# Query splits two groups ahead, a ring of two for the K products, early prompt rows, and a compression loop that runs through sample boundaries

## The reference, cut to what matters

```python
q, kvc_rows, kvs_rows, kvw_rows, gl, u = project_in(h, p['w_in'])
kv_c, cmp_end = cmp_finish(cmp_partials(kvc_rows, p['w_cmp']), p['pe_cmp'], p['w_cmp'])
# cmp_partials: blocks of 16 rows times weights, two halves r
return jnp.einsum('bnsxhd,xrsde->rbnxhe', sub, w)
# for each sample the rows of the compressed branch come through a page table
kvc_past = cache_kv_cmp[layer, page_table].reshape(bd, past_len, 2, N_KV_HEADS, HEAD_DIM)
```

## Time and profile before

| | us |
|---|---|
| median of 3 runs | 1994.75 |
| lowest and highest run | 1992.07, 1998.62 |
| profiled execution, its own time | 1998.57 |
| span of the profiled execution, first to last instruction | 1996.9 |
| PE busy in the span | 1787.3 (90%) |
| projection, from its first matmul to its last | 36.25 to 287.4 |
| compression, from its first transpose to the first of the attention | 288.2 to 427.2 |
| attention, to the first transpose of the next stage | 427.2 to 888.9 |
| rest: SSM, output projection, FFN, final norm | 888.9 to 1996.9 |

### The profile page before, as it was taken

One profiled execution on the slowest core, in us unless ns is written; L12 is line 12 of the kernel. 1 busy time (PEld: TensorE's weight loads), 2 busy tenths in 40 slices (PEclk: granted clock), 3 DMA queues, 4 the chain that ended last, 5 costly groups with the idle time before them and its releaser, 6 DMA issues. The chain is left out here.

```text
span 1996.9 us, 27094 instructions
## 1 busy us (share of the span) xinstructions
PE 1787.3 (90%) x10875; PEld 1502.0 (75%) x10876; DVE 915.0 (46%) x1404; ACT 567.9 (28%) x876; POOL 307.6 (15%) x265
## 2 busy tenths in 40 slices
PE   5999788856998999886869979999999999999988
PEld 4655778854555554545649979999999999999977
DVE  3456004673544443417121055555555555555554
ACT  4000013553443343320221133232222222222222
POOL 0000000022212211210011012222222222222210
PEclk8999897977999999896989979999999999999999
DMA  6312414401333322536010021112111111211102
GB/s 257 65 43 107 157 49 153 164 39 53 96 95 112 121 85 86 197 134 199 4 63 22 1 75 40 55 32 63 32 60 35 34 61 32 63 32 57 37 11 90
DMA packets 94796, 155.15 MB, mean 78 GB/s; under 512 B 19670, under 2 KB 72446, under 8 KB 92366
## 3 DMA queue, kind: packets, MB, share of 16 engines
q1 hardware_dynamic: 81200, 93.82, 14.7%
q0 software_dynamic: 12672, 58.73, 8.8%
q10 hardware_dynamic: 848, 1.54, 0.3%
HBM read 133.61 MB, written 24.83 MB: 79 GB/s over the span
## 5 line engine op out<-in xcount | busy, mean ns | idle before, releaser
L2224 PE MATMUL ps<-h_up,w_split 128*128 128x344 f32 x2112 | 403.5, 323 | 9.2 <-DVE h_rest L2394 7.4
L2403 DVE TENSOR_TENSOR xT<-ps,xT 128x1032 f32<-128x1032 f32 x176 | 216.9, 1233 | 316.8 <-PE ps L2224 316.8
L2224 PEld LDWEIGHTS ps<-h_up,w_split 128*128 128x128 f32 x2112 | 344.1, 189 | 20.1 <-issue 16.5
L2224 PE MATMUL ps<-gated,wd_split 128*128 128x344 f32 x1584 | 266.8, 324 | 3.0 <-POOL wd_split L2380 2.1
L2224 PEld LDWEIGHTS ps<-gated,wd_split 128*128 128x128 f32 x1584 | 250.5, 188 | 12.7 <-DVE xT L2403 7.8
L2224 PE MATMUL ps<-h_rest,w_split 128*128 128x344 f32 x1056 | 225.0, 321 | 0.0
L2224 PEld LDWEIGHTS ps<-h_rest,w_split 128*128 128x128 f32 x1056 | 179.5, 190 | 0.0
L2410 DVE SCALAR_TENSOR_TENSOR cv<-hu,ccol,cv 128x1024 f32<-128x1024 f32 x88 | 142.7, 1622 | 16.4 <-ACT cv L2322 10.7
L2320 ACT ACTIVATE hu<-ps 128x1032 f32<-128x1032 f32 x44 | 45.4, 1033 | 331.9 <-PE ps L2224 331.9
L2360 POOL TENSOR_TENSOR w_split<-w_raw,w_split 128x1024 fp32r<-128x1024 f32 x44 | 107.0, 2433 | 188.1 <-ACT w_split L2305 188.1
L1601 DVE TENSOR_REDUCE top<-ps 128x1 f32<-128x384 f32 (+4 forms) x124 | 71.3, 586 | 139.4 <-PE ps L1226 73.6
(11 more groups left out here) (436 smaller groups left out, 2514.1 us busy)
## 6 DMA issues: line engine op xcount, KB each, us to landing
w_raw<-in_w_up SPq DMA_DIRECT2D x44, 512.0 KB, 6.1
wd_raw<-in_w_down SPq DMA_DIRECT2D x22, 512.0 KB, 3.6
unit<-in_cache_kv_win POOLq DMA_DIRECT2D x16, 512.0 KB, 4.6
x_kept<-xT SPq DMA_DIRECT2D x1, 4128.0 KB, 25.4
xT<-x_kept SPq DMA_DIRECT2D x1, 4128.0 KB, 19.6
xtok<-in_x_prompt SPq DMA_DIRECT2D x2, 2048.0 KB, 8.1
w_qu<-in_w_in SPq DMA_DIRECT2D x2, 2048.0 KB, 8.6
w_out_sb<-in_w_out SPq DMA_DIRECT2D x4, 1024.0 KB, 5.0
```

What stands on the lines that cost most here:

```text
L2224: mm = pe.matmul(k.ps[:, bank + c, 0:TG], w(wn), x(xn)[:, c * TG:c * TG + TG], start=start and m == 0, stop=stop and m == 2)
L2403: dve.tensor_tensor(x, k.ps[:, bank:bank + 3, 0:TG], x, ALU.add).then_inc(added, 1)
```

## The change

1. **Splits.** "split" of groups 0 and 1 stand at the head of `ORDER`; "split" of g + 2 stands in group g ahead of "value" of the selected branch, instead of at the head of group g + 1.
2. **K products.** `kk_stage` has two places, each with a semaphore of its own; the copy of product x waits for the store of product x - 2. The eight loads of `w_c` go from SP's list to POOL's, into another place in SBUF, behind `cw_made` and the store `pb_kept`.
3. **Prompt rows.** Tile 0 has a place of its own (`tile0`), and SP loads it at the end of its list in the projection, behind the K products' stores and `cw_kept`. `uc_early` moves to the place of sample buffer 0. So gather 2, which writes there, waits for the store `u_kept`.
4. **Compression.** PE, ACT and DVE run one loop over all 72 fills; the combine of tile j - 1 comes after the copy of fill 1 of tile j. Copies of `uc_early` alternate between ACT and DVE.

```diff
+    k.kk_out = [nc.alloc_semaphore(f"kk_out{n}") for n in range(2)]
...
-            for x in range(2):
-                for r in range(2):
-                    for s2 in range(2):
-                        src = k.dram["w_cmp"][0][x, r * SUB + s2:(r + 1) * SUB:2].rearrange("s d e -> d s e")
-                        sp.dma_start(k.w_c[HD * s2:HD * s2 + HD, x, :, r, :], src).then_inc(k.wc_loaded, 16)
             for x in range(KK_FILLS):
                 sp.wait_ge(kk_added, x + 1)
-                sp.dma_start(k.kk_kept[:, 8 * P * x:8 * P * x + 8 * P], k.kk_stage[:].rearrange("c g q -> c (g q)")).then_inc(k.kk_out, 16)
+                sp.dma_start(k.kk_kept[:, 8 * P * x:8 * P * x + 8 * P], k.kk_stage[:, x % 2].rearrange("c g q -> c (g q)")
+                             ).then_inc(k.kk_out[x % 2], 16)
+
+            sp.wait_ge(k.cw_out, 16)
+            for x in range(2):
+                for h in range(NKV):
+                    sp.dma_start(k.tile0[NSUBP:NSUBP + 2, :, 2 * x + h, :],
+                                 k.dram["pe_cmp"][0, x].rearrange("(r s) d -> r s d", r=2)).then_inc(k.prompt_in, 16)
+            sp.wait_ge(*k.cmp_rows_stored)
+            sp.dma_start(k.tile0[0:NSUBP].rearrange("n s c d -> n (s c d)"),
+                         k.dram["p_kv_cmp"][0, 0].rearrange("(n s) x h d -> n (s x h d)", s=SUB)).then_inc(k.prompt_in, 16)
...
+            pool.wait_ge(cw_made, 1)
+            pool.wait_ge(k.pb_out, 16)
+            for x in range(2):
+                for r in range(2):
+                    for s2 in range(2):
...
+                        pool.dma_start(k.w_c[HD * s2:HD * s2 + HD, x, :, r, :], src).then_inc(k.wc_loaded, 16)
...
-                    if x:
-                        act.wait_ge(k.kk_out, 16 * x)
-                    else:
+                    if x >= 2:
+                        act.wait_ge(k.kk_out[x % 2], 16 * (x // 2))
+                    elif x == 0:
...
-            sp.wait_ge(u_moved, 8)
-            sp.wait_ge(k.kk_out, 16 * 4)
+            sp.wait_ge(u_act, 4)
+            sp.wait_ge(u_dve, 4)
             sp.dma_start(k.u_kept, k.uc_early[:].rearrange("p g n -> p (g n)")).then_inc(k.u_spilled, 16)
...
-                if j >= 2:
+                if j == 2:
+                    pool.wait_ge(k.u_spilled, 16)
+                if j >= 3:
 
                     pool.wait_ge(transposed, FILLS * (j - 1))
...
+            for F in range(FILLS * (NB + 1) + LAG):
+                j, f = divmod(F, FILLS)
+                if j <= NB:
...
+                    if F >= 4:
+
+                        pe.wait_ge(moved_act, F - 3)
+                        pe.wait_ge(moved_dve, F - 3)
+                    turn(j, f, width.get(j, P))
+                if F >= LAG:
+                    M = F - LAG
+                    j, f = divmod(M, FILLS)
...
+                    pe.wait_ge(moved_act, M + 1)
+                    pe.wait_ge(moved_dve, M + 1)
+                    multiply(j, f, width.get(j, P))
...
+                ins.then_inc(moved, 1)
+                if f == LAG - 1 and j:
+                    finish(j - 1, width.get(j - 1, P))
+            finish(NB, P)
...
-    ORDER = [("split", 0)] + [("look", 0, *s) for s in looks_of(0)] + [("merge", 0), ("turn", 0)]
+    ORDER = [("split", 0), ("split", 1)] + [("look", 0, *s) for s in looks_of(0)] + [("merge", 0), ("turn", 0)]
...
-        if nxt:
-            ORDER.append(("split", g + 1))
...
             ORDER += [("merge", g + 1), ("turn", g + 1)]
+        if g + 2 < len(GROUPS):
+            ORDER.append(("split", g + 2))
         ORDER.append(("value", g, SEL))
```

More of the change, by code:

```diff
@@ L693, in after @@
                     dve.wait_ge(kk_copied, x + 1)
-                    dve.tensor_tensor(k.kk_stage[:, :, 0:GC], k.kk_stage[:, :, 0:GC], k.dd[:, 8 * x:8 * x + 8], ALU.add
+                    dve.tensor_tensor(k.kk_stage[:, x % 2, :, 0:GC], k.kk_stage[:, x % 2, :, 0:GC], k.dd[:, 8 * x:8 * x + 8], ALU.add
                                       ).then_inc(kk_added, 1)
@@ L736, in plan_early @@
     k.Bin, o = at("Bin", [P, 2, NJ, GC], F32, o)
+    after_powers = o
     k.ldt, o = at("ldt", [NJ, 2], F32, o)
@@ L745, in plan_early @@
     k.bt_stage, _ = at("bt_stage", [P, 2, 512], F32, 9216 + 18432)
-    k.kk_stage, _ = at("kk_stage", [GC, 8, P], F32, 9216 + 18432)
-    k.w_c, _ = at("w_c", [P, 2, SUB // 2, 2, HD], F32, 9216 + 24576)
-    k.uc_early, _ = at("uc_early", [P, G, NCH], F32, 9216)
+    k.kk_stage, _ = at("kk_stage", [GC, 2, 8, P], F32, 9216 + 18432)
+    k.w_c, end = at("w_c", [P, 2, SUB // 2, 2, HD], F32, tail + 6144)
+    assert end <= after_powers, (end, after_powers)
+    k.tile0, _ = at("tile0", [P, SUB, 2 * NKV, HD], F32, 9216)
+    k.uc_early, _ = at("uc_early", [P, G, NCH], F32, k.off_mix)
     k.Cin, _ = at("Cin", [GC, 2, G, PS], F32, k.off_u)
@@ L845, in _ @@
                 if x >= 4:
[L846 removed]
+                    pe.wait_ge((u_act, u_dve)[x % 2], x // 2 - 1)
                 for a in range(4):
@@ L851, in _ @@
             pe.wait_ge(k.wc_loaded, 8 * 16)
-            for j in range(NB + 1):
-                n = width.get(j, P)
-                if j == 0:
-                    pe.wait_ge(prompt_in, 5 * 16)
-                else:
-                    pe.wait_ge(tile_in[j % 2], 16 * ((j + 1) // 2))
-                for f in range(FILLS + 2):
-                    F = FILLS * j + f
-                    if f < FILLS:
-                        if F >= 4:
-                            pe.wait_ge(moved_act, F - 3)
-                            pe.wait_ge(moved_dve, F - 3)
-                        turn(j, f, n)
-                    if f >= 2:
-                        if f == 2 and j < 2:
-                            pe.wait_ge(u_moved, 6 + 2 * j)
-                        if f == 2 and j >= 2:
-                            pe.wait_ge(combined, j - 1)
-                        pe.wait_ge(moved_act, F - 1)
-                        pe.wait_ge(moved_dve, F - 1)
-                        multiply(j, f - 2, n)
@@ new lines, in move @@
+        def move(eng, copy, h, moved, finish):
+            for F in range(FILLS * (NB + 1)):
+                j, f = divmod(F, FILLS)
+                n = width.get(j, P)
+                eng.wait_ge(transposed, F + 1)
+                if F >= 4:
+                    eng.wait_ge(multiplied, F - 3)
+                rows = k.ps[HD * h:HD * h + HD, f % 4, :].rearrange("p (a s n) -> p s a n", a=2, s=2)
+                for s2 in range(2):
+                    ins = copy(k.rowsT[HD * s2:HD * s2 + HD, f % 4, h, :, 0:n], rows[:, s2, :, 0:n])
+                ins.then_inc(moved, 1)
+                if f == LAG - 1 and j:
+                    finish(j - 1, width.get(j - 1, P))
+            finish(NB, P)
@@ L912, in _ @@
             link = Link(dve, c_link)
+            for x in range(1, 8, 2):
+                dve.wait_ge(u_turned, x + 1)
+                dve.tensor_copy(k.uc_early[:, 4 * x:4 * x + 4, :].rearrange("p g n -> p (g n)"), k.ps[:, 4 + x % 4, :]
+                                ).then_inc(u_dve, 1)
             dve.memset(k.kcp[:], 0.0)
```

51 lines of the change are left out of this document (20 added, 31 removed).

## The result

| | changed kernel | before, on the same chip |
|---|---|---|
| median | 1938.72 us (1935.96 to 1943.00, 4 runs) | 1996.68 us (1992.07 to 2000.28, 4 runs) |
| ratio | 0.9713, 95% interval 0.9684 to 0.9741 | |
| profiled execution: time, span | 1938.17, 1936.5 us | 1998.6, 1996.9 us |

The change takes 57 us off (52 to 63 by the interval). First the stretches of the changed kernel by stage: the `u` jobs of the projection, the compression, the attention up to its first score, from there to the transposes of `oacc`, and the rest. The columns are those of the earlier trace rows.

A forecast was written before the change was run, and what follows sets the result against it. PE's work at its granted clock plus its idle time was taken to bound compression and attention. K products -12, compression -31.8 and splits -11 sum to -54.8 us: 1998.6 becomes 1943.8, the median 1994.75 becomes 1940, range 1927 to 1955.

The forecast's parts named there:

- Rival 4: Projection: POOL writes `w_c`'s 4096 pieces so slowly that the kernel gets slower, up to 2036 us; chance 0.025.
- Tile 0: Compression: tile 0 follows the `U` transposes at clock 1.00 instead of 0.50, gain 8.7 us, bounds 0 and 8.7.
- rival 1: Compression held by a late gather 2 or tile 0 at the lower clock, loss 5 to 13 us, say 1950; chance 0.14.
- Gathers: Compression: a new PE wait of 2.5 us for gather 2 plus 1.5 at lower clock, 4 us lost, bounds 0 and 9.
- Boundaries: Compression: seven tiles shorter by 1.86 us, the eighth's start by about 0.4; gain 13.4 us, bounds 9 and 14.9.
- rival 3: Attention: waits only change their name, ACT late for `oT` or the exponential, gain 0 to 4, 1947 to 1951; chance 0.11.
- the bound of 18: Attention: upper bound of the splits' gain, 18 us, if falls of the clock behind the `q_up` waits go too.

The follow-up runs named there:

- e2: Changed kernel with one place for the K products as before, `w_c` still loaded by POOL; 1955.12 us, ratio 0.9776.
- e3: Changed kernel with the eight loads of `w_c` back on SP ahead of the K stores, two K places kept; 1942.81 us, ratio 0.9725.
- e5: Changed kernel with the prompt's rows asked for at the start of the compression again; 1957.13 us, ratio 0.9804.
- e1: Changed kernel with the queries split as before, at the head of the group before their own; 1955.87 us, ratio 0.9785.
- e8: Changed kernel with POOL making the second parts of `q` for groups 0 and 1 ahead of its first five unit fetches; 1939.81 us, ratio 0.9706.
- e4: Changed kernel with the compression's loop ending at each sample again, as before; 1952.66 us, ratio 0.9780.
- e7: Changed kernel with the compression's multiplies three fills behind the turns instead of two; 1938.65 us, ratio 0.9702.
- b1: Kernel before the change with nothing but the new splits, two groups ahead; 1980.98 us, ratio 0.9915.
- e10: e9 with tile 0 turned and multiplied 128 columns wide instead of 66; 1929.40 us, ratio 0.9663.
- e9: e8 with each of DVE's two sample weighings waiting only for its own half of the 64 small gate-row loads; 1934.06 us, ratio 0.9666.

## Why the prediction was right, and where its terms were off

The median came out at 1938.72 us where 1940 was forecast. That it is so near is in part luck. The sum was made against the profiled execution, and there it is 5.6 us short (1943.8 forecast, 1938.17 measured). The 1940 was then counted from a median of 1994.75, where the kernel before measured 1996.68 beside the changed one. The mechanism held in all four parts, but for the clock in tile 0 and for a clock term missing from the splits; the sizes were off as follows.

*K products: -12 forecast, -12.7 measured.* The mechanism is shown by e2 (wait back, 9.2 us) and e3. The store landed in time with 3.3 us to spare, where 0.4 us of wait was forecast. The rule weighed in the prediction (the Trainium skill, DMA: Bandwidth & Descriptors, "Issuing engines are not separate DMA queues": issuing elsewhere saves only the sequencer's time, usually small beside the transfer itself) agrees in part. With `w_c` back on SP (e3) the store landed some 5 us later, so the move was not small for the store; only 1.4 us of that reached PE.

*Moved loads: nothing forecast, nothing lost.* POOL takes 0.71 us for each issue of `w_c`, where 2.2 was worked out in proportion to the pieces from its plain load. Rival 4 lay far off.

*Prompt: -13.7 for the wait, and it is all gone;* e5 brings 14.3 of it back.

*Tile 0: the first term that was mis-sized.* 8.7 us were forecast for it at clock 1.00, a gain of 8.7. In the profiled run it took 12.4, because the clock fell in the middle of it, so the gain there was 4.9 (17.35 less 12.43). This is the clock part of rival 1, come true in part (3.8 of the 8.7). The forecast is not wrong for every execution: in e1 tile 0 took 9.99 us, of which 1.00 was a wait for gather 1, so 8.99 without it (7.71 of work and the new wait of 1.28).

*Gathers: +4 forecast, 0 measured in the changed kernel,* since a slow tile 0 covers them. Where the narrow tile 0 ran at 1.00 under the new loop, PE waited for tiles for 1.7 us (e1) and 2.9 (e8), near the forecast's 2.5, but for gathers 1 and 2 and not for gather 2 alone. The errors of this term and of tile 0, 4 and 3.8, cancel; rival 1 had noted that the two don't add up.

*Boundaries: -13.4 forecast.* What is left of the stage's 29.0 is 29.0 - 13.7 - 4.9 = 10.4, so 3.0 less. The period itself came out as forecast, 10.90 against 10.84, a gain of 1.8 at each of the later tiles. The difference is tile 1: its first fills run at the lower level behind tile 0, and it takes 303.79 - 290.38 = 13.4 us where it took 12.9 before. With tile 0 at 1.00 in both (e4 and e1) the loop is worth 13.9 us by the stage; the whole of e4 has 13.4. The remainder of 0.26 us for each tile, 0.2 in the forecast, is PE's wait for a copy, and e7 removes it.

*Splits: the term that was mis-sized most, 11 forecast, 18.9 measured (17.2 when made alone, b1).* The working of 11 was the idle time only: 13.0 of waits, less a little. Idle time did fall by 9.5: the 13.0 went, and 3.4 came back under other names (`sd` 7.0 to 7.5 us, the transpose of `top` 4.2 to 4.8, the unit's fetch 3.7 to 5.0, the looks' wait for `top` 1.9 to 2.9), about a quarter, where rival 3 had nearly all come back; neither the exponential nor the copy of `oT`, which the prediction had named as late next, is among them. What the 11 left out, though it stood in the bound of 18 (which the 18.9 pass by a little), is the clock: PE's busy time for the same matmuls fell by 9.4 us when the waits went. e1 and b1 show that this part comes and goes with the splits.

*The sum:* -54.8 forecast, -60.6 in the three touched stages: 7.9 more from the splits, 0.7 more from the K products, 2.8 less from the compression. The rest of the 60.4 is +1.2 and -1.1 us in stretches that the change does not touch, and such a size means nothing: the stretch behind the attention, the same in all, took from 1106.6 us (e10) to 1114.3 (e9).

## What to carry to other kernels

When an engine's waits are taken away, price the clock with them: compare its busy time for the same instructions with and without the waits, and count that as well as the idle time. Before a wait is shortened, look for the transfer that is late for someone who is not yet waited for (here the 64 small loads, late by 1.0 us for DVE): it takes the gain back as soon as the wait is gone. To split its semaphore by who needs which part gave it back here (e9). Parts that act on separate gaps of the bounding engine added up here, so each could be priced from its own stretch.

## What the runs showed of the hardware

- The granted clock fell from 1.00 to 0.50 in tile 0 of the changed kernel, near 283 us, while PE had been busy without a gap since 280.15, and rose again in tile 1, near 296; the same instructions stayed at 1.00 in e1. The Trainium skill, TensorE: Matmul & The Clock Gate, section "What's actually happening", has sustained activity release the lower level. The rise in tile 1 agrees; the fall in tile 0 does not.
- Sixty-four issues of three numbers each took SP 42.55 us in e8, 0.66 us each, nearly as much as POOL's 0.71 us for a load of 128 KB in 512 pieces.
- In the changed kernel the store of `cw_kept` (2304 KB), issued in 0.44 us at 199.50, landed 29.6 us later, and the first K store behind it took 14.5 us where the median of the four was 3.4.
